# Up projection in pairs of token halves: seven products on two alternating bank sets, and the surrounding queues reordered

## What is computed

```python
x = x + mixed @ w_out                       # stage "out": output projection and residual
h = rmsnorm(x, g_ffn)
up = h @ w_up                               # stage "up": 1024 -> 2 * 2816 channels
ext = concatenate([prefix, up])             # then a causal depthwise conv of width 3
c = conv(ext, conv_w) + conv_b
gate, val = split(c, 2)
y = x + (silu(gate) * val) @ w_down         # stage "down": 2816 -> 1024
return rmsnorm(y, g_final)                  # and the last rows of several states
```

## Time and profile before

| | |
|---|---|
| median of the runs | 1502.4 us |
| the profiled execution | 1501.96 us, span 1500.1 us |
| mean granted TensorE clock | 0.958 |
| TensorE busy | 1396.7 us (93%) |
| weight loads busy (beside the matmuls) | 1352.0 us |
| VectorE busy | 838.3 us (56%) |
| ScalarE busy | 577.0 us (38%) |
| GpSimd busy | 150.3 us (10%) |
| HBM traffic | 150 MB, 100 GB/s over the span |
| output projection, up stage, row stage, 32 units | about 546 to 651, 651 to 1203, 1203 to 1299, 1299 to 1489 us |

### The profile page before, as it was taken

The page is one execution under the profiler, slowest core; times in us unless marked ns, Lnnn a source line. Parts: engine busy times, 40 slices in busy tenths (PEclk is TensorE's granted clock), DMA queues, the critical chain, the costliest instruction groups (busy, mean ns, idle before and its releaser), DMA issues.

```text
span 1500.1 us, 22653 instructions
## 1 busy us (share of the span) xinstructions
PE 1396.7 (93%) x9199; PEld 1352.0 (90%) x9199; DVE 838.3 (56%) x1081; ACT 577.0 (38%) x925; POOL 150.3 (10%) x296
## 2 busy tenths in 40 slices
PE   4999999999999998987999999999999989998996
PEld 4999888999999988887989899898989989998996
DVE  6123544544465432365777777777777656532643
ACT  5112234444441133354344444444444345342532
POOL 1000100000000011112121121212212110000000
PEclk8999989999999998988999999999999999999998
DMA  9111102122254422312212121221212169538562
GB/s 255 47 43 47 34 30 82 63 73 72 73 162 133 144 73 88 103 44 57 73 58 80 51 87 59 71 73 58 87 44 87 69 233 333 159 88 260 143 201 78
DMA packets 183508, 150.57 MB, mean 100 GB/s; under 512 B 16824, under 2 KB 169996, under 8 KB 183379
## 3 DMA queue, kind: packets, MB, share of 16 engines
q1 hardware_dynamic: 183418, 149.33, 31.9%
HBM read 118.43 MB, written 31.98 MB: 100 GB/s over the span
## 4 chain that ended last, share of the span: by engine, by line
PE 33%; issue 5%; POOL 5%; ACT 3%; DVE 3%; DMA 2%; SPq 1%; ACTq 0%; POOLq 0%; DVEq 0%
PE PS L1180 18%; PE PS L1324 10%; PE PS L1277 4%; POOL tpack L2426 3%; POOL ext L2429 2%; DVE ext L2174 2%; ACT conv_gate L1624 2%; DMA da_raw<-act_scratch 1%; DMA wm_raw<-in_w_down_dram 1%; ACT s_hi L1361 1%; PE PS L1308 1%; POOL tpack L2427 0%; SPq L742 0%; ACT r_copy L1361 0%; DVE wm_lo L2248 0%
## 5 line engine op out<-in xcount | busy, mean ns | idle before, releaser
L1180 PE MATMUL PS<-y_lo,s_hi 128*128 128x272 f32 x528 | 153.2, 290 | 0.0
L847 PE MATMUL PS<-h_hi,up_hi 128*128 128x364 f32 (+1 forms) x600 | 138.9, 340 | 0.0
L847 PE MATMUL PS<-h_hi,up_lo 128*128 128x364 f32 (+1 forms) x600 | 133.1, 330 | 0.0
L847 PE MATMUL PS<-h_lo,up_hi 128*128 128x364 f32 (+1 forms) x600 | 133.1, 330 | 0.0
L1324 PE MATMUL PS<-a_hi,wm_hi 128*128 128x384 f32 (+1 forms) x352 | 115.9, 329 | 7.3 <-DVE wm_lo L2248 5.8
L1324 PE MATMUL PS<-a_lo,wm_hi 128*128 128x384 f32 (+1 forms) x352 | 114.3, 325 | 0.0
L1324 PE MATMUL PS<-a_hi,wm_lo 128*128 128x384 f32 (+1 forms) x352 | 114.2, 325 | 0.0
L847 PEld LDWEIGHTS PS<-h_hi,up_hi 128*128 128x128 f32 x600 | 102.0, 190 | 10.9 <-issue 10.0
L1180 PE MATMUL PS<-yb_hi,s_hi 128*128 128x272 f32 x352 | 107.1, 304 | 4.2 <-DVE s_lo L2006 4.2
L1746 DVE TENSOR_TENSOR up_lo<-raw,up_hi 128x1024 fp32r<-128x1024 f32 x42 | 54.0, 1286 | 101.7 <-ACT up_hi L1361 101.7
L1180 PE MATMUL PS<-yb_hi,a_hi 128*128 128x272 f32 x352 | 102.4, 291 | 3.8 <-DVE a_lo L2006 3.8
(11 more groups left out here) (297 smaller groups left out, 3569.0 us busy)
## 6 DMA issues: line engine op xcount, KB each, us to landing
raw<-in_w_up_dram SPq DMA_DIRECT2D x44, 512.0 KB, 3.8
wm_raw<-in_w_down_dram SPq DMA_DIRECT2D x32, 704.0 KB, 4.7
raw<-in_w_in_dram SPq DMA_DIRECT2D x22, 512.0 KB
act_scratch<-conv_val SPq DMA_DIRECT2D x22, 512.0 KB, 2.6
dw_raw<-in_w_down_dram SPq DMA_DIRECT2D x22, 512.0 KB, 4.1
gates_scratch<-gate_st SPq DMA_DIRECT2D x16, 546.0 KB, 2.7
gates<-gates_scratch SPq DMA_DIRECT2D x16, 546.0 KB, 4.6
y_scratch<-xT SPq DMA_DIRECT2D x8, 544.0 KB, 3.9
```

The source lines that it names most:

```text
L847: ins = pe.matmul(PS[:, 3 * s + piece, 0:width], w[:, first_k + n, :], x[:, k, first:first + width], start=(n == 0 and q == 0), stop=(n == ...
L1180: ins = pe.matmul(PS[:, bank, 0:HALF], w[:, k, :], f(q % 2, k), start=start and k == 0 and t == 0, stop=k == KH - 1 and t == 2, skip_group ...
```

## The change

TensorE runs each product for both token halves in a row. The shared accumulator of p1, p6, p7 and p4 is bank q % 2 for odd j and bank 6 + q % 2 for even j, so that the C21 copies of block j-1 need not be done before p1 of block j begins. ScalarE's and VectorE's rounds are reordered to match, the two taps after the first are no longer adjacent, and on GpSimd the copy that first_tap waits for goes ahead of the tpack copies.

```diff
+def chain_bank(q):
+    return (q % 2 if q // 2 % 2 else 6 + q % 2)
             def p1(q):
                 if q >= 2:
-                    pe.wait_ge(c21_done, q - 1)
-                product("a11", q, q % 2, True)
+                    if q < 4:
+                        pe.wait_ge(aux_free, AUX_SSQ + 1)
+                    else:
+                        pe.wait_ge(c21_done, q - 3)
+                    if q == 4:
+                        pe.wait_ge(aux_free, AUX_RMS + 2)
+                product("a11", q, chain_bank(q), True)
# TensorE, up stage
-            for q in range(2, NHALF):
-                p6(q); p4(q - 1); p5(q); p3(q - 1)      (one call a line in the file)
-                if q + 1 < NHALF: p1(q + 1)
-                p7(q); p2(q)
+            for j in range(1, NFF):
+                a, b = 2 * j, 2 * j + 1
+                p1(a); p1(b); p3(a - 2); p3(b - 2); p6(a); p6(b)
+                if j == 1:
+                    pe.wait_ge(c21_done, 2)
+                    spread_rms(0); spread_rms(1)
+                p5(a); p5(b); p7(a); p7(b); p2(a); p2(b); p4(a); p4(b)
# ScalarE, up stage, order of a round for j > 1
+  take_c21(a-1), split a12, split a22, take_p1(a), first_tap(j-1,0), take_p1(b), split s4, take_v(a),
+  first_tap(j-1,1), take_v(b), split a11(j+1), split s2(j+1), silu(j-1), take_r(a), split s1(j+1),
+  take_r(b), take_c21(a), split s3(j+1)
# VectorE, up stage, order of a round for j > 1
+  lo s3, scale_rows(j-1,0), lo a12, lo a22, product(j-2), add_c12(a-2), second_tap(j-1,0),
+  add_c12(b-2), scale_rows(j-1,1), lo s4, third_tap(j-1,0), weight sums 1, 2, 4 of j+1, lo a11(j+1),
+  lo s2(j+1), add_c22(a), second_tap(j-1,1), add_c22(b), lo s1(j+1), third_tap(j-1,1),
+  add_c11(a), add_c11(b), weight sum 3 of j+1
# j = 1: rms_row is copied and take_v(a), take_p1(b) come before first_tap(0,0); the order of ScalarE
# is take_v(2), split s4(1), rms_row, first_tap(0,0), first_tap(0,1), take_v(3)
# GpSimd
                 samp = row[:, EXT_S:EXT].rearrange("p (b t) -> p b t", b=DEC_B)
+                pool.tensor_copy(spaced(row)[:, :, CSTATE:], samp).then_inc(spread, 1)
                 pool.tensor_copy(tpack[:, 0:CSTATE, ch], row[:, EXT_S - CSTATE:EXT_S])
                 pool.tensor_copy(tpack[:, CSTATE:NROW, ch]..., samp[...])
-                pool.tensor_copy(spaced(row)[:, :, CSTATE:], samp).then_inc(spread, 1)
# SP: the store of act row j moves from the round after product(j) was made to the next order
-                if 1 <= j < NFF - 1:
-                    store_act(j - 1)
+                if j >= 2 and j + 1 < NFF:
+                    store_act(j - 2)
# SP, output projection: the store of y goes ahead of the weight chunk
+                sp.wait_ge(acc_free, FILL_OUT - FILL_BRANCH + m + 1)
+                sp.dma_start(y_dram[m], xT[:, 0:T]).then_inc(y_spilled, 16)
                 if m < 4:
                     c = CHUNK_OUT + m + 4
                     load_chunk(c, c % 2, out_views(m + 4, m % 2))
-                if m == 6:  load_val(0)   ... if m == 7:  load_gate(0)
+                if m == 4:  load_val(0)   ... if m == 5:  load_gate(0)
-                sp.wait_ge(acc_free, FILL_OUT - FILL_BRANCH + m + 1)
-                sp.dma_start(y_dram[m], xT[:, 0:T]).then_inc(y_spilled, 16)
# TensorE, output projection: steps before which x is transposed
+            project(0, 0, 12, 18, ready=...)
+            for m in range(1, KD - 1):
+                project(m, m % 2, 9, 18)
+            project(KD - 1, (KD - 1) % 2, 3, 14, read=mx_read)
# SP, units: the four loads for the last segment
-                    for g in range(2): load_act(a2_raw, 2, g)        (u == 11; g = 2, 3 at u == 12)
+                if u == 8:  load_act(a2_raw, 2, 0)
+                if 11 <= u <= 13:  load_act(a2_raw, 2, u - 10)
```

More of the change, by code:

```diff
@@ L1114, in _, with project @@
                 branch(i * 2 + 3, 1)
-            def project(m, half, ready=None, read=None):
+            def project(m, half, first, second, ready=None, read=None):
                 pe.wait_ge(w_lo, m + (CHUNK_OUT + 1))
@@ L1131, in project @@
                 gemm(half, CHUNK_OUT + half, 0, range(KD), mx_hi, mx_lo,
-                     {12: lambda: aux_round(m * 2 + AUX_X, turn_x), 18: lambda: aux_round(m * 2 + (AUX_X + 1), turn_x_last)},
-                     ready)
-            project(0, 0, ready=lambda k: pe.wait_ge(mix_lo_done, k + 1))
-            for m in range(1, KD):
-                project(m, m % 2)
+                     {first: lambda: aux_round(m * 2 + AUX_X, turn_x),
+                      second: lambda: aux_round(m * 2 + (AUX_X + 1), turn_x_last)}, ready, read)
+            project(0, 0, 12, 18, ready=lambda k: pe.wait_ge(mix_lo_done, k + 1))
+            for m in range(1, KD - 1):
+                project(m, m % 2, 9, 18)
+            project(KD - 1, (KD - 1) % 2, 3, 14, read=mx_read)
             def token_squares():
@@ L1529, in b_hi, with y_part @@
                     copy(yb_hi[:, m, 0:T], y[:, m, 0:T]).then_inc(b2_hi, 1)
[L1531 to L1536 removed]
+            def y_part(rows, n):
+                return y[:, rows, 0:T].rearrange("p k (h n t) -> p h k n t", h=2, n=2)[:, :, :, n, :]
+            FIRST, LAST = slice(0, KH - 1), slice(KH - 1, KH)
+            for m in range(KD - 1):
+                copy_x(m)
+                copy_x_last(m)
+                weighted(m)
+                if m == KD - 2:
+                    b_hi(m)
+                squares(m)
                 if m < KD - 2:
                     split_hi(m % 2, (m - m % 2) + (CHUNK_OUT + 2))
[L1539 removed]
                     b_hi(m)
[L1541 to L1545 removed]
+            act.wait_ge(acc_full, FILL_OUT + KD - 1)
+            split_slot("a11", 0)
+            copy_x(KD - 1)
+            act.wait_ge(t23_sub, KH - 1)
+            act.wait_ge(mx_read, 2)
+            copy(t2_hi[:, :, FIRST, :], y_part(FIRST, 0)).then_inc(t2_hi_done, 1)
+            copy_x_last(KD - 1)
+            act.wait_ge(mx_read, 4)
+            copy(t3_hi[:, :, FIRST, :], y_part(FIRST, 1)).then_inc(t3_hi_done, 1)
+            split_slot("s1", 0)
+            act.wait_ge(t4_sub, 1)
+            act.wait_ge(mx_read, 6)
+            copy(t4_hi[:, :, FIRST, :], t4_first[:, :, :, :]).then_inc(t4_hi_done, 1)
+            act.wait_ge(acc_full, FILL_OUT + KD)
+            split_slot("a12", 0)
+            split_slot("s2", 0)
+            weighted(KD - 1)
             def take_p1(q):
@@ L1562, in take_r @@
                     act.wait_ge(c22_done, q)
[L1563 removed]
+                copy(r_copy[:, :], PS[:, chain_bank(q), 0:HALF]).then_inc(r_copied, 1)
             def take_c21(q):
@@ L2222, in _ @@
                     split_slot_lo("s1", j + 1)
-                product(j - 1)
-                if j + 1 == NFF:
-                    row_lo(0)
-            add_c22(NHALF - 1)
-            add_c11(NHALF - 1)
+                third_tap(j - 1, 1)
+                add_c11(a)
+                add_c11(b)
+                if j + 1 < NFF:
+                    weight_sum_3(j + 1)
             row_lo(1)
+            scale_rows(NFF - 1, 0)
+            product(NFF - 2)
+            add_c12(NHALF - 2)
             add_c12(NHALF - 1)
-            scale_rows(NFF - 1, 0)
@@ L2249, in unit_lo @@
                     .then_inc(wm_low, 1)
-            for k in range(4, NFF):
+            for k in range(5, NFF):
                 row_lo(k)
```

413 lines of the change are left out of this document (225 added, 188 removed).

## The result

The changed kernel takes 1407.17 us (median of 4 runs, 1402.28 to 1412.31) against 1502.36 for the kernel before beside it: ratio 0.9364, 95% interval 0.9326 to 0.9401. The forecast was 1410.4. The profiled execution of the new kernel has a span of 1404.5 us and took 1406.26; TensorE is busy 97% of it.

A forecast was written before the change was run, and what follows sets the result against it. TensorE, busy 93%, bounds the kernel, so only its waits and clock can be won. Gains of 66.3 (up stage), 18.8 (output projection), 4.4 (row stage) and 2.5 (units) sum to 92.0 us: 1410.4, range 1392 to 1446.

The forecast's parts named there:

- A round is 21.3 us, at clock 1.00: Up stage, steady rounds: 21.3 us each, 0.2 above TensorE's floor, no fall of the clock; bounds 21.1 to 21.8.
- The sum for VectorE, 21.1 us: Up stage round: VectorE's 18.3 us busy plus 2.1 and 0.7 idle give 21.1, level with TensorE's 21.09.
- The two slacks: Up stage round: take_p1(b) ends 0.3 us before p6(b) needs it, take_v(b) 1.2 before p7(b).
- The old wait goes because its cover grows from one product to four: Up stage: the 1.76 us wait for r_copy in each round disappears, covered by four products instead of one.
- Head, 12.3 us over its work: waits 1.1 + 4.6 + 2.0 and 4.6 of clock: First rounds of the up stage: waits for rms_row, p7(3), p6(5), plus three clock falls; 12.3 us, bounds 3 to 25.
- Output projection, 18.8: Output projection: xT's store ahead of the weight chunk load removes four waits; gain 18.8 us, bounds 11 to 19.
- Row stage, 4.4, and the old up stage: Row stage's 22 steps fall from 96.5 to 92.0 us, gain 4.4; old up stage 551.1, new 484.8, gain 66.3.
- Units, 2.5: Units: the second late wait, 2.48 us, goes as two segment loads precede its weights, not four; gain 2.5, bounds -3, 4.
- Rival 1: Up stage: VectorE and GpSimd become the bound, rounds 21.8 us; 1420 to 1435, say 1427; chance 0.17.
- Rival 2: Up stage: the clock falls though no wait is left, ten more falls, 15 us: 1425; chance 0.09.
- Rival 3: Up stage: take_r(a) behind silu still comes too late for TensorE, rounds stay at 23.9 us; 1462; chance 0.07.
- Rival 4: Up stage: act row's store, behind two weight loads, lands late, delaying p7(b); landing at 17.5 gives 1526 us; chance 0.05.

The follow-up runs named there:

- Run 2: Kernel before with one ScalarE line moved: take_r(2j) right after take_p1(2j+1), ahead of first_tap and silu, no pairing: 1441.07 us, ratio 0.9598.
- run 4: Changed kernel with one bank set for the accumulator p1, p6, p7 and p4 share, token squares in aux, take_c21(1) at head's end: 1408.87 us, ratio 0.938.
- run 1: Kernel before with one SyncE edit: for output chunks 0 to 3, xT's store ahead of the next weight chunk's load: 1479.41 us, ratio 0.9856.
- Run 10: Changed kernel with the first three output stores of the units each issued one unit later: 1400.6 us, ratio 0.933.
- run 5: Changed kernel with GpSimd's two tpack copies put back ahead of the spaced copy that first_tap waits for: 1436.36 us, ratio 0.9558.

## Why the prediction was right, and where it was wrong

- *A round is 21.3 us, at clock 1.00.* It is 21.04. Product for product 1.503 us, so TensorE alone sets it; the 0.2 that I had put above its floor (4 us in all) wasn't spent. The sum for VectorE, 21.1 us, was too high: GpSimd's copy of the samples, put at 0.64, took 0.24 beside a VectorE that stood idle, and the gap before the second tap left 1.7 us idle and not 2.1. So the two engines weren't quite level.
- *The two slacks.* p6(b) has 0.8 in most rounds instead of 0.3; p7(b) has 1.6 in most instead of 1.2. The order of VectorE and GpSimd was read rightly from the earlier trace rows. What I had wrong is that nothing else could end last before take_v(b): in five rounds of 18 it is the act row's store, with down to 0.3 us of slack. Its 2.6 us from the earlier trace rows were taken for a store issued ahead of the weight loads; behind them it takes 4.9.
- *The old wait goes because its cover grows from one product to four.* The wait went, but the reason holds only halfway. Run 2 has the cover of one product and run 4 one bank set, and neither waits. What the wait needed was take_r(a) ahead of first_tap and silu. In the changed kernel take_r(a) still stands behind silu, and there the longer cover is what it lives on; it is one of two ways, not a need. I had no line in the forecast for "the same gain from one moved copy", though the earlier trace rows named the copy.
- *Head, 12.3 us over its work: waits 1.1 + 4.6 + 2.0 and 4.6 of clock.* It is 54.8 us for 43.5 of matmul work, 11.3 over. p7(3) waits 4.42 (forecast 4.6), rms_row 1.11. The 2.0 at p6(5) never came: first_tap gate of that round began 5.7 us after p1(4), against 5.1 in a steady round, so VectorE was about 0.5 behind and not 2.9. Where it caught up isn't shown. Instead 1.62 stands at p6(2), and 1.4 in three small pieces. The sum was right partly by chance: 8.6 of waits against 7.7, and 2.7 for the clock against 4.6.
- *Output projection, 18.8.* 18.9, with all the steps as told; run 1 shows it alone.
- *Row stage, 4.4, and the old up stage.* The end of the old up stage was misread: 1202.52 lies 18 matmuls inside the first row step. The old row stage took 99.8 us and not 96.5, so 8.0 us were gained and not 4.4; the old up stage took 547.8 and not 551.1. The new stages came out as told, 483.1 us for 484.8 and 91.8 for 92.0, the row stage without a wait. The total didn't suffer: what was counted too much in one stage was missing in the other.
- *Units, 2.5.* This step failed: nothing was gained. The wait of 2.48, which it was about, is gone. But the first segment load, moved to u = 8, made the weights of an earlier unit 3.4 us late, and the ring of store, scaling and weights brought that to TensorE as a wait for yt of 3.12. The bound of -3, "the first load, at u = 8, delays a unit", had named just this; I took it for the edge and not for the case. What I had not seen at all is the ring, which the kernel before has as well. Run 10 shows that with the store out of it both waits go.
- *Not in the forecast:* the last round's 2.72 us (4.5 with what follows it), also an entry in SyncE's list that moved past another, which I had priced only for the steady rounds.
- *Rival 1* was near: with the copies in the other order (run 5) the kernel takes 1436, just above the 1420 to 1435 given for it, and by another route than I had put there (1.3 us a round in two short waits, without a fall of the clock). *Rival 2* is refuted: 380 us of rounds without a wait at clock 1.00. *Rival 3* also: no wait for r_copy. *Rival 4* is real in one round; in the others it has slack, 0.3 us in the tightest.

Misses of 1 to 5 us lay on both sides (rounds and head better by 6, units and last round worse by 7, the start better by 4), and so the total came out 3 us off. That it is so near is partly chance.

## What to carry to other kernels

When one wait returns in every round, look first at what stands ahead of the late instruction on its own engine. Moving one copy of 0.37 us past two long ones gave 61.9 of the 95 us here, without touching the schedule of the matmuls. And when a list in order is rearranged, price each entry that itself waits, in the first and the last round as well as in the steady one: both of the change's losses were transfers with nothing wrong in them. One stood behind a load that had to wait, the other behind a store that had to wait and a load put in between.

## What the runs showed of the hardware that was not expected

- A wait of 0.80 us in each round left the granted clock at 1.00 (run 5, the window above), where waits of 1.76 us were followed by a stretch at 1.2 GHz in about ten rounds of 19 (granted clock 0.50 from 854.50 to 856.50, behind the wait that ends at 853.14).
- A GpSimd copy of 128 x 2 elements takes 0.19 us or 1.28 us, according to the VectorE instruction that runs beside it; three copies in a row each wait out one such instruction in turn.
- A store of 512 KB lands in 2.6 us when issued first, in 4.9 behind two weight loads of the same size, and in 5.7 with one more store of its size ahead of it (medians): the second neighbour cost much less than the first two.
- The same code up to the output projection took from 525.6 to 534.4 us in twelve executions, with granted clocks of 0.86 to 1.00 in its first 50 us that don't go with the times: 0.6% of the kernel's time that no edit made.
